# Two-layer hybrid block on one core: the tail of layer 0's feed-forward and the head of layer 1, token tile by token tile

## What is computed

```
y  = (silu(x @ w1) * (x @ w3)) @ w2          # layer 0's feed-forward
h  = h + gate * rmsnorm(y, g_post)           # sandwich norm, gate, residual
u  = rmsnorm(h, g_pre) * (1 + scale) + shift # layer 1's norm and modulation
p  = u @ w_in                                # layer 1's input projection
```

## Time and profile before

| | |
|---|---|
| median of 3 runs | 2373.79 us (2369.2 to 2374.8) |
| the profiled execution | 2372.3 us |
| its span in the profile | 2370.5 us |
| its mean granted TensorE clock | 0.964 |
| TensorE busy | 94% of the span |
| VectorE (DVE) busy | 61% |
| ScalarE (ACT) busy | 49% |
| last feed-forward matmul to first matmul of layer 1's input projection | 1083.05 to 1114.89 us of the span |

### The profile page before, as it was taken

The page is one execution under the profiler, slowest core; times in us unless marked ns, Lnnn a source line. Parts: engine busy times, 40 slices in busy tenths (PEclk is TensorE's granted clock), DMA queues, the critical chain, the costliest instruction groups (busy, mean ns, idle before and its releaser), DMA issues.

```text
span 2370.5 us, 37936 instructions
## 1 busy us (share of the span) xinstructions
PE 2222.8 (94%) x15802; PEld 1835.8 (77%) x15802; DVE 1437.6 (61%) x2086; ACT 1157.0 (49%) x1603; POOL 121.3 (5%) x94
## 2 busy tenths in 40 slices
PE   6998989999999999995988899889999999999996
PEld 4767768788777888884766799778888888888885
DVE  2125667444343222334466566378999989999896
ACT  3224344323232222324254344267878778787785
POOL 0000441000000000000014300000000000000000
PEclk8999999999999999997989999979999999999998
DMA  8883002332212322220300154259989899898994
GB/s 332 327 334 139 1 2 92 142 107 72 89 65 100 107 89 93 103 74 36 107 1 2 53 220 167 115 216 350 359 333 374 340 350 359 331 374 342 348 361 159
DMA packets 63327, 448.31 MB, mean 189 GB/s; under 512 B 7217, under 2 KB 8241, under 8 KB 9521
## 3 DMA queue, kind: packets, MB, share of 16 engines
q1 hardware_dynamic: 60880, 434.86, 48.3%
q10 hardware_dynamic: 2272, 10.97, 1.2%
HBM read 443.71 MB, written 2.10 MB: 188 GB/s over the span
## 4 chain that ended last, share of the span: by engine, by line
PE 86%; DVE 4%; ACT 4%; issue 2%; DMA 2%; PEld 1%; POOL 1%; SPq 0%; ACTq 0%; DVEq 0%; PEldq 0%; POOLq 0%
PE bank L1135 11%; PE bank L1236 10%; PE bank L629 9%; PE bank L610 7%; PE bank L612 7%; PE bank L611 7%; PE bank L1249 5%; PE bank L770 4%; PE bank L489 4%; PE bank L1172 4%; PE bank L715 3%; PE bank L1155 2%; PE bank L727 2%; PE bank L562 1%; PE bank L647 1%
## 5 line engine op out<-in xcount | busy, mean ns | idle before, releaser
L2003 DVE TENSOR_TENSOR wsp_l<-ring,wsp_h 128x1024 fp32r<-128x1024 f32 x528 | 639.9, 1222 | 40.1 <-ACT wsp_h L1335 9.0
L1335 ACT CAST wsp_h<-ring 128x1024 fp32r<-128x1024 f32 x528 | 555.2, 1054 | 151.4 <-PE bank L612 89.7
L610 PE MATMUL bank<-wsp_h,xTs_h 128*128 128x512 f32 x704 | 283.9, 403 | 2.5 <-DVE xTs_l L1995 2.5
L612 PE MATMUL bank<-wsp_h,xTs_l 128*128 128x512 f32 x704 | 276.3, 393 | 0.0
L611 PE MATMUL bank<-wsp_l,xTs_h 128*128 128x512 f32 x704 | 275.1, 391 | 0.0
L2536 DVE TENSOR_TENSOR dsp_l<-ring,dsp_h 128x1024 fp32r<-128x1024 f32 x66 | 80.8, 1225 | 241.7 <-ACT dsp_h L1736 241.7
L1736 ACT CAST dsp_h<-ring 128x1024 fp32r<-128x1024 f32 x66 | 69.1, 1048 | 257.5 <-PE bank L1236 182.6
L1135 PE MATMUL bank<-u_hi,gsp_h 128*128 128x512 f32 (+1 forms) x512 | 174.2, 340 | 1.2 <-DVE arena L2460 1.2
L1135 PE MATMUL bank<-x_lo,gsp_h 128*128 128x512 f32 (+1 forms) x512 | 171.7, 335 | 0.0
L1135 PE MATMUL bank<-u_hi,gsp_l 128*128 128x512 f32 (+1 forms) x512 | 171.5, 335 | 0.0
L2103 DVE TENSOR_TENSOR ring_lo<-ring,win_hi 128x1024 fp32r<-128x1024 f32 x44 | 56.1, 1278 | 169.7 <-ACT win_hi L1445 167.1
(11 more groups left out here) (348 smaller groups left out, 4386.7 us busy)
## 6 DMA issues: line engine op xcount, KB each, us to landing
ring<-in_moe_tiles_dram SPq DMA_DIRECT2D x264, 1024.0 KB, 4.9
ring<-in_ada_tiles_dram SPq DMA_DIRECT2D x48, 1024.0 KB, 11.0
ring<-in_ffn_tiles_dram SPq DMA_DIRECT2D x33, 1024.0 KB, 4.8
ring<-in_gate_tiles_dram SPq DMA_DIRECT2D x32, 1024.0 KB, 5.9
ring<-in_in_tiles_dram SPq DMA_DIRECT2D x22, 1024.0 KB, 4.9
arena<-in_branch_tiles_dram ACTq DMA_DIRECT2D x8, 1024.0 KB, 8.6
ring<-in_out_tiles_dram SPq DMA_DIRECT2D x8, 1024.0 KB, 4.8
halfc<-in_halfc_dram SPq DMA_DIRECT2D x1, 1040.0 KB, 19.0
```

The source lines that it names most:

```text
L610: pe.matmul(o, xTs[0][:, kk, :], whi[:, k, :], start=(kk == 0), stop=False)
L612: mm = pe.matmul(o, xTs[1][:, kk, :], whi[:, k, :], start=False, stop=(kk == KD - 1))
L1335: act.copy(wsp[0][:, g % 4, :], half_slot(MOE0, g)).then_inc(s.gq_o.up, 1)
L2003: v.tensor_tensor(wsp[1][:, g % 4, :], half_slot(MOE0, g), wsp[0][:, g % 4, :], ALU.subtract).then_inc(s.gq_pt.up, 1)
```

## The change

1. TensorE's loop over the inner blocks is cut at block 19. Blocks 0 to 18 run as before. For the last three blocks the token tile becomes the outer loop: tile 0 takes blocks 19, 20 and 21, then tile 1, and so on. `f_out` is raised after each tile. The hidden parts of block 21 go to `hsp0`, and ACT and DVE prepare them ahead of the weights of block 21.
2. Squares, mean, root, reciprocal and residual run tile by tile, in an interleaved order, and so do layer 1's squares, mean, root, reciprocal and scaling. DVE multiplies y by the gate before the root is there, and one `scalar_tensor_tensor` then multiplies by 1/rms and adds to `h`.
3. The transposes run in two groups, tiles 0 and 1 into banks 0 to 3 and tiles 2 and 3 into banks 4 to 7, tile by tile inside a group (`next_T`). Evacuation is by group too: each bank holds two channel blocks of one stream; ACT takes banks 0, 1, 4, 5 and DVE banks 2, 3, 6, 7 (`next_part`).
4. At the head of layer 1 the casts, subtractions and evacuations stand in another order. Layer 0's head is as before.

The core of the diff (signal counts, wrappers and the unchanged branch for layer 0 cut):

```
@@ TensorE
+            def next_T(s, below, g):
+
+                pe.wait_ge(*below.po_h2(2 * g + 2))
+                for i, t in enumerate(PARTS[0][g]):
+                    pe.wait_ge(*s.xs1(t + 1))
+                    for b in range(4):
+                        for k, c in part_rows(0, g, b):
+                            mm = transpose(bank[part_banks(0, g) + b][:, c.start + P * i:c.start + P * (i + 1)],
+                                           xs_next[:, t, P * k:P * (k + 1)])
+                        if i:
+                            mm.then_inc(s.tp1.up, 1)
...
-                    for f in range(NF):
-                        q = 2 * NF + f
-                        pe.wait_ge(*g_wlo(MW + q + 1))
+                    for f in range(NF - 3):
+                        pe.wait_ge(*g_wlo(MW + 2 * NF + f + 1))
                         pe.wait_ge(*g_xlo(2 * KD + f + 1))
...
+                    for t in range(NT):
+                        for f in range(NF - 3, NF):
+                            if t == 0:
+                                pe.wait_ge(*g_wlo(MW + 2 * NF + f + 1))
+                                pe.wait_ge(*g_xlo(2 * KD + f + 1))
+                            mm = second_stage(f, t)
+                            if t == NT - 1:
+                                mm.then_inc(g_used.up, 1)
+                        if t < NT - 1:
+                            mm.then_inc(s.f_out.up, 1)
...
-                    pe.wait_ge(*s.po_h2(2))
@@ ScalarE
-                    for q in range(2, 3 * NF):
+                    for q in range(2, 3 * NF - 1):
                         ffn_weight(q)
...
+                    hidden_high(NF - 1)
+                    ffn_weight(3 * NF - 1)
+                    above = sig[1]
+                    for t in range(2):
+                        post_squares(s, t)
+                        post_root(s, t)
+                    for t in range(2):
+                        next_square(s, above, t)
+                        post_squares(s, 2 + t)
+                        next_root(s, t)
+                        if t == 0:
+                            post_root(s, 2)
+                    next_square(s, above, 2)
+                    post_root(s, 3)
+                    next_part(above, 0, 0)
+                    next_root(s, 2)
+                    next_square(s, above, 3)
+                    next_root(s, 3)
+                    next_part(above, 0, 1)
...
+                    weight_high(0)
+                    for b in range(2):
+                        next_part(s, 1, b)
+                        input_high(2 * b)
+                        input_high(2 * b + 1)
+                    for k in range(4, KD):
+                        input_high(k)
@@ VectorE
-                for t in tiles:
-                    for hf in range(2):
-                        c = slice(512 * hf, 512 * (hf + 1))
-                        link(v.scalar_tensor_tensor(area(A_TR + 512 * hf, 512), bank[2 * t + hf][:, :],
-                                                    stat[:, 1, 8 + t:9 + t], GB[:, t // 2, c], ALU.mult, ALU.mult))
-                        ins = v.tensor_tensor(h[:, t, c], h[:, t, c], area(A_TR + 512 * hf, 512), ALU.add)
-                    ins.then_inc(g_h.up, 1)
+            def post_add(s, t):
+
+                gated = area(6 * TOK, 2, 512) if t % 2 else sil0
+                for hf in range(2):
+                    v.wait_ge(*s.po_sq2(2 * t + hf + 1))
+                    v.tensor_tensor(gated[:, hf, :], bank[2 * t + hf][:, :], GB[:, t // 2, 512 * hf:512 * (hf + 1)], ALU.mult)
+                x = stat[:, 1, 8 + t:9 + t]
+                link(v.tensor_tensor(x, stat[:, 1, 2 * t:2 * t + 1], stat[:, 1, 2 * t + 1:2 * t + 2], ALU.add))
+                mean_eps(x, D, s.po_ss2)
+                v.wait_ge(*s.po_rs2(t + 1))
+                link(v.reciprocal(x, x))
+                for hf in range(2):
+                    c = slice(512 * hf, 512 * (hf + 1))
+                    ins = v.scalar_tensor_tensor(h[:, t, c], gated[:, hf, :], x, h[:, t, c], ALU.mult, ALU.add)
+                ins.then_inc(s.po_h2.up, 1)
+
+            def next_norm(s, above, t):
+
+                v.wait_ge(*above.ssq1(t + 1))
+                x = stat[:, 0, t:t + 1]
+                mean_eps(x, D, s.nx_ss)
+                v.wait_ge(*s.nx_rs(t + 1))
+                link(v.reciprocal(x, x))
+                v.tensor_scalar(xs_next[:, t, :], h[:, t, :], x, None, ALU.mult).then_inc(above.xs1.up, 1)
...
-                    post_add(s.po_sq2, s.po_ss2, s.po_rs2, s.gb_ok2, s.po_h2, tiles)
+                    hidden_low(NF - 1)
+                    ffn_weight(3 * NF - 1)
+                    above = sig[1]
+                    v.wait_ge(*s.gb_ok2(4))
+                    post_add(s, 0)
+                    post_add(s, 1)
+                    next_norm(s, above, 0)
+                    post_add(s, 2)
+                    next_norm(s, above, 1)
+                    post_add(s, 3)
+                    next_norm(s, above, 2)
+                    next_norm(s, above, 3)
+                    for b in (2, 3):
+                        next_part(above, 0, b)
...
+                    weight_low(0)
+                    input_low(0)
+                    input_low(1)
+                    for b in (2, 3):
+                        next_part(s, 1, b)
+                    for k in range(2, KD):
+                        input_low(k)
```

More of the change, by code:

```diff
@@ L1239, in _, with second_stage @@
                     pe.wait_ge(*s.f_hid(NF - 2))
-                    for f in range(NF):
-                        q = 2 * NF + f
-                        pe.wait_ge(*g_wlo(MW + q + 1))
+                    def second_stage(f, t):
+                        for x, w in ((0, 0), (0, 1), (1, 0)):
+                            for hf in range(2):
+                                mm = pe.matmul(bank[2 * t + hf][:, :], hidden_part(x, f)[:, P * t:P * (t + 1)],
+                                               dsp[w][:, (2 * NF + f) % 3, 512 * hf:512 * (hf + 1)],
+                                               start=(f == 0 and x == w == 0), stop=(f == NF - 1 and x == 1))
+                        return mm
+                    for f in range(NF - 3):
+                        pe.wait_ge(*g_wlo(MW + 2 * NF + f + 1))
                         pe.wait_ge(*g_xlo(2 * KD + f + 1))
@@ L1402, in gate_rows, with post_squares, post_root, next_root @@
                     act.copy(rows[:, streams[n // 2], 512 * (n % 2):512 * (n % 2 + 1)], bank[first + n][:, :]).then_inc(g_ok.up, 1)
[L1404 to L1411, removed]
+            def post_squares(s, t):
+                act.wait_ge(*s.f_out(t + 1))
+                for hf in range(2):
+                    if t or hf:
+                        act.wait_ge(*s.po_sq2(2 * t + hf))
+                    act.activation(squared_y, bank[2 * t + hf][:, :], ACT.Square,
+                                   accum_out=stat[:, 1, 2 * t + hf:2 * t + hf + 1]).then_inc(s.po_sq2.up, 1)
+            def post_root(s, t):
+                root(stat[:, 1, 8 + t:9 + t], s.po_ss2, s.po_rs2, t + 1)
+            def next_root(s, t):
+                root(stat[:, 0, t:t + 1], s.nx_ss, s.nx_rs, t + 1)
+            def next_square(s, above, t):
+                act.wait_ge(*s.po_h2(t + 1))
+                square(above.ssq1, t, t, 0)
+            def next_part(s, g, b):
+                act.wait_ge(*s.tp1(4 * g + b + 1))
+                for k, c in part_rows(0, g, b):
+                    ins = act.activation(uT[:, k, part_columns(0, g)], bank[part_banks(0, g) + b][:, c], ACT.Identity,
+                                         scale=scl[:, 1, 0, k, 1 - g:2 - g], bias=shift[:, 1, 0, k, 1 - g:2 - g])
+                ins.then_inc(s.u_odd.up, 1)
             for l in range(DEPTH):
@@ new lines, in next_norm, with next_part @@
+            def next_norm(s, above, t):
[5 more added lines that the diff above has]
+                v.tensor_scalar(xs_next[:, t, :], h[:, t, :], x, None, ALU.mult).then_inc(above.xs1.up, 1)
+            def next_part(s, g, b):
+                v.wait_ge(*s.tp1(4 * g + b + 1))
+                for k, c in part_rows(0, g, b):
+                    ins = v.tensor_scalar(uT[:, k, part_columns(0, g)], bank[part_banks(0, g) + b][:, c],
+                                          scl[:, 1, 0, k, 1 - g:2 - g], shift[:, 1, 0, k, 1 - g:2 - g], ALU.mult, ALU.add)
+                ins.then_inc(s.u_even.up, 1)
```

101 lines of the change are left out of this document (51 added, 50 removed).

## The result

| | before | changed |
|---|---|---|
| median of the first comparison | 2371.56 us (4 runs, 2369.2 to 2374.8) | 2351.11 us (4 runs, 2349.46 to 2353.87) |
| ratio, 95% interval | | 0.9918 [0.9899, 0.9937] |
| span of the profiled execution | 2370.5 us | 2347.9 us |
| mean granted clock | 0.964 | 0.973 |

A forecast was written before the change was run, and what follows sets the result against it. TensorE, busy 94%, was taken as the bound, with time won only in its 31.9 us hole after the feed-forward. Profiled 2372.3 - 15.2 = 2357.1, plus 1.5 to the median, gave 2358.6 us; range 2353 to 2366.

The forecast's parts named there:

- nothing absorbed later: Stages after the hole: gain passes through whole; the rival, absorption there, predicted 2370 us or more, chance 0.05.
- cost of nothing for block 21's weights: End of the feed-forward: block 21's weights, needed sooner, ready with 0.4 us margin, so no stall was costed.
- rival of a load at each change of function: ACT on the tile chains: 14 x 1.28 = 18 us of table loads, leaving 1 us gain, 2373 us; chance 0.03.
- step 2: Tile chains on ACT and DVE after the feed-forward's tiles: DVE sets the pace, scaling ends 12.8 us sooner, at 1093.7.
- step 3: Transposes, evacuation, layer 1's first projection products: first matmul 17.5 us sooner, 25th at 1105.9 instead of 1121.1, gain 15.2 us.
- 12 slow matmuls of layer 0's start: Layer 1's input projection: first 12 matmuls 0.43 us apart at the low clock, as in layer 0; gain 15.2 us.
- clock high at once: Start of layer 1's input projection: without slow matmuls, the second half slot's weights (1104.7) limit it; gain 16.3 us.
- 2.5 us for scatter around a median of 2373.8: Total time: allowance for a median's scatter, added to the 16.3 and 12.9 us bounds, giving 2355 to 2363.5 us.

The follow-up runs named there:

- the gate product: Gate product put back behind root and reciprocal, tile by tile otherwise as in the changed kernel; ratio to the kernel before 0.9921 [0.9894, 0.9948].

## Why the prediction was right and wrong

**Right in mechanism.** TensorE without a gap to the end of the feed-forward, one table load, DVE setting the pace together with its waits for ACT's roots, a shorter hole and nothing absorbed later all came as written. Counted from tile 2's end, the last scaling was forecast 14.9 us later and ended 13.7 later. The cost of nothing for block 21's weights held: ACT cast them at 1064.77, DVE was done at 1067.09, and the row of matmuls has no gap. The rival of a load at each change of function is refuted: eight roots alternate with squares and evacuations from 1071.61 to 1089.74, and there is one load. The price of a switch in the Trainium skill (ScalarE: Activation LUTs, "What ACT_TABLE_LOAD costs"), about 2.66 us, of which 1.38 a drain, is not what this trace shows: the load began 0.02 us behind the end of ACT's instruction before it (1070.30), took 1.28 us, and the root began 0.01 us behind its end.

The steps that failed are two terms of the sum, both too long.

**Wrong in size, the tile chains (step 2): 1.2 us too long.** I added lengths of rows where starts are what counts. On DVE, in

```profile
1081.67 1.41 DVE L2030 SCALAR_TENSOR_TENSOR h<-arena,stat,h 128x512 f32<-128x512 f32 x2
...
1083.00 0.14 DVE L1965 TENSOR_SCALAR stat<-stat 128x1 f32<-128x1 f32 x1
```

the next operation starts 0.08 us before the row of 1.41 ends, and so at nearly each of DVE's hand-overs to itself, four or five a tile. About half of the 1.2 us lies on ACT, where the chain runs twice. From tile 2's root to the root that the scaling of tile 1 waits for (timeline of ACT, the rows of reading the accumulator left out):

```profile
1081.23 0.20 ACT L1421 ACTIVATE stat<-stat 128x1 f32<-128x1 f32 x1 [2.47 <-DVE stat L1965]
1081.34 1.04 ACT L1417 ACTIVATE arena<-h 128x1024 f32<-128x1024 f32 x1
...
1082.38 0.58 ACT L1443 ACTIVATE arena<-bank 128x512 f32<-128x512 f32 x1
...
1083.67 0.19 ACT L1421 ACTIVATE stat<-stat 128x1 f32<-128x1 f32 x1
```

it is 2.44 us, where the forecast's lengths (0.21, 1.16 and 1.44) add up to 2.8; the pass from tile 2's end to the first scaling was 0.25 shorter than forecast too, most of it on ACT.

**Wrong in size, the first matmuls (step 3): 1.3 us too long.** I took the 12 slow matmuls of layer 0's start, one of two bounds. Six or none were slow in the changed kernel's three executions. From first to 25th matmul it was 7.2 us each time, and 8.5 in the forecast. The bound "clock high at once" would have been right even with six matmuls at the low clock: the second half slot's low part sets it. In the changed kernel (timeline of DVE):

```profile
1096.80 3.69 DVE L2193 TENSOR_TENSOR x_lo<-uT,u_hi 128x512 fp32r<-128x512 f32 x6
1100.41 1.21 DVE L2200 TENSOR_TENSOR ring_lo<-ring,win_hi 128x1024 fp32r<-128x1024 f32 x1
```

It is done at 1101.6, and the 25th matmul begins at 1101.8. Together, 15.2 + 1.2 + 1.3 = 17.7.

**Wrong in width.** The prediction let all other stages pass unchanged and allowed 2.5 us for scatter around a median of 2373.8. The medians of the kernel before in the comparisons are 2370.9 to 2372.2, 1.6 to 2.9 us lower. The three medians of the changed kernel are 2351.1, 2356.0 and 2351.3 us: the forecast of 2358.6 misses all three, the lower end of 2353 misses two. The gain by ratio is 16 to 20 us, around the seam's 17.7 to 18.6. Of the 7.5 us between 2358.6 and the first result of 2351.1, 2.5 are the two steps above, 2.2 are the lower median of the kernel before (2371.56), and 2.8 belong to no step: in another job the same kernel came out 4.9 us higher. That the first gain was 20.4 us and not 17.7 lies within this scatter and is not credited to the change.

**What stays open.** In which execution the clock is low at the projection's start is not explained: of the eleven profiled executions with the tile-by-tile seam (the first result included) it was high in six, one of them that of the kernel with idle matmuls, and low in five. The clock records of the changed kernel say only where it stood: low from 6.3 to 16.5 us after the start of the feed-forward's last matmul in the execution with six slow matmuls, and from 5.2 to 12.0 us in the other two, where the projection's first matmul came at 13.6. How much of the scatter in the late stretch comes from the clock is read from such comparisons and not isolated by a run, and the scatter ahead of the feed-forward has no cause here.

## What to carry to other kernels

When a hole on the critical engine is filled by two other engines, split the work so that the first piece is ready early, and check which engine's total then sets the end; here DVE's chain of 20 to 21 us does, of which 3.4 to 4.4 are its waits for ACT, and starting it 8.5 us earlier is worth 7.3. An edit that shows no effect can be hidden by a wait elsewhere on the same chain, as is likely for the gate product. Work out such chains from start to start, and try both limits of a stretch together before concluding that one is worthless. A gain of a few microseconds is better read from a stretch that repeats to 0.1 us between executions than from total times that scatter by 5.

## What was not expected

- A stretch of identical code with many short waits took 437.4 to 443.4 us, and everything up to layer 0's feed-forward 713.2 to 721.1 us, over twelve of the thirteen profiled executions of these kernels.
- The seam of the kernel before varies more (38.5 and 39.4, with 3 and 8 slow matmuls) than the changed one's (20.8 three times, with 0 or 6): where DVE sets the pace, up to six slow matmuls are hidden. Nine were not, in the run with the roots first.
